# Two ways to the expert activations: half of the tokens by gathered rows, half by dense plain products, and the up product in a stage of its own

## The chip, the cores and the metric

One core of a Trainium2 chip runs the whole program. The metric is the device time of one execution in microseconds, the median of three runs. Four engines compute (PE is TensorE, DVE is VectorE, ACT is ScalarE, POOL is GpSimd), SP is the queue that issues DMA transfers, and each engine executes its own instructions in order and waits on semaphores.

## The reference

The reference is three layers on x [256 tokens, 1024]: a first block (attention, then an expert layer), and two mixers with windowed attention. Only the expert layer is touched. For one token with normalised row h it computes, for each of 8 heads:

```
q      = h @ w_query                          # 2 halves of 128 per head
sc     = q . sub_keys                         # 128 scores per half
top 16 of each half -> 256 pair sums -> top 16 of them: (expert, score)
gates  = softmax(best 16 scores)
act    = gelu(h . expert_down[expert])        # rows of 1024
out   += sum gates * act * expert_up[expert]
```

There are 16384 experts (128 x 128), and 8 x 16 = 128 chosen ones ("slots") for each token. expert_down and expert_up are 64 MB each in fp32.

## The kernel before, in words

It never gathers. It treats the experts as 128 chunks of 128 rows. For every chunk and all 256 tokens it computes the dense activations gelu(down_chunk . h), multiplies them by a table of gates that is zero where a token did not choose the expert, and adds weights x up_chunk into four PSUM banks. The transposed normalised rows are `whole` (fp32, [128, 8, 256]) and `hT` (the same split in a high and a low fp32r part). `plain` products are fp32 matmuls; `three_passes` (L228) replaces one fp32 product by three fp32r ones of high and low parts.

The expert layer runs in three parts, each a block with a barrier between.

`route_phase` (L1379): 16 steps, one for each head half. PE makes the queries (three passes over 8 k-blocks, L1468) and the scores (L1480); ACT and POOL split the query weights; DVE takes the top 16 of each half straight from PSUM (`top16`, L1521), both token halves (t = 0 and 1) in one step. After the steps DVE takes the top 16 of the pair sums for each head (L1542), finds the two digits of each chosen expert by comparing with 16 candidates (L1560 to L1578) and normalises the gates. Under this PE runs `EARLY` = 24 dense chunks in plain fp32 (class `Ahead`, L1278: 8 matmuls with 256 columns for a chunk).

`spread_phase` (L1599): the slots are transposed, and for 32 groups of 8 tokens DVE builds two one-hot matrices of [128 slots, 8, 128] (L1661, L1664), PE multiplies them token by token (L1706) and thereby scatters the gates into [128, 128] tables, ACT copies them out, and DVE merges them with the chunks whose activations exist. PE runs 14 more plain chunks in between.

`experts_phase` (L1733): the up products of all 128 chunks (`add`, L1777: 12 matmuls with 512 columns: two token halves, two halves of D, three passes). For the first 38 chunks the activations exist. For the other 90 (`both`, L1793) PE also makes the down product in three passes, 24 matmuls with 256 columns, whose operands ACT and DVE split; ACT applies gelu and DVE multiplies by the gates. Every chunk also needs ACT and DVE to split 1024 columns of the up rows (L1813, L1843).

All loads go out of SP's queue in program order: a down chunk as two halves of 256 KB into two buffers, an up chunk in the same way. POOL issues no DMA.

After it the two mixers run as they are; they are not touched.

## Time and profile before

| | |
|---|---|
| median of 3 runs | 1572.26 us (1571.95 to 1572.6) |
| profiled execution | span 1569.9 us; its whole time is not shown, so the 2.4 us between span and median are taken as what lies around it |
| PE busy | 1531.3 us, 98% of the span |
| DVE busy | 1013.8 us, 65% |
| ACT busy | 699.4 us, 45% |
| POOL busy | 42.0 us, 3% |
| DMA | 239.30 MB, mean 152 GB/s |
| granted PE clock | 1.00 in nearly all of the span (mean 0.999) |

A busy PE is one with a matmul in flight, not one at its peak. Shares are over the whole span; the stages of the expert layer are told apart by time below.

### The profile page before, as it was taken

The numbers are of one execution on the slowest core, as the hardware profiler recorded it, in microseconds if no ns is written. First come the engines' busy times: TensorE is split into PE (matmuls) and PEld (weight loads), VectorE is DVE, ScalarE is ACT, GpSimd is POOL, SyncE is SP. The second block draws the span as 40 slices with busy tenths as digits, with TensorE's granted clock in tenths as the row PEclk, the third lists the DMA queues.
The fourth block names the chain that finished last, engine by engine and source line by source line (L and its number), as shares of the span: only waits on it lengthen the run. The fifth ranks groups of instructions, "written<-read, shape, count | busy, mean of one in ns | idle before, by whom it ended". The sixth has DMA issues, their size and how long they took to land. (4 is left out here: it accounts for less than half of the span.)

```text
span 1569.9 us, 29197 instructions
## 1 busy us (share of the span) xinstructions
PE 1531.3 (98%) x9047; PEld 1338.6 (85%) x9047; DVE 1013.8 (65%) x2452; ACT 699.4 (45%) x1484; POOL 42.0 (3%) x42
## 2 busy tenths in 40 slices
PE   7998999999999999999999999999999999999998
PEld 4665798889878899999999999979999999759994
DVE  4666589989867666666666666665555555247762
ACT  2443241223344444444444444446666666326651
POOL 0000260000000000000000000000000000000000
PEclk9999999999999999999999999999999999999999
DMA  7420244422265555555555555557544444317630
GB/s 290 157 105 1 65 145 146 150 86 68 82 205 189 187 187 187 187 187 187 187 187 187 187 187 187 187 174 229 175 149 148 148 147 148 94 33 231 168 106 28
DMA packets 163511, 239.30 MB, mean 152 GB/s; under 512 B 41712, under 2 KB 91376, under 8 KB 161904
## 3 DMA queue, kind: packets, MB, share of 16 engines
q1 hardware_dynamic: 163440, 238.42, 46.8%
q8 instruction: 37, 0.61, 0.2%
q14 instruction: 34, 0.28, 0.1%
HBM read 237.09 MB, written 1.29 MB: 152 GB/s over the span
## 5 line engine op out<-in xcount | busy, mean ns | idle before, releaser
L232 PE MATMUL projection<-hT_high,down_low 128*128 128x256 f32 x720 | 203.8, 283 | 0.0
L231 PE MATMUL projection<-hT_low,down_high 128*128 128x256 f32 x720 | 203.7, 283 | 0.0
L230 PE MATMUL projection<-hT_high,down_high 128*128 128x256 f32 x720 | 203.3, 282 | 0.0
L230 PE MATMUL experts_acc<-experts_uh,experts_wh 128*128 128x512 f32 x512 | 200.6, 392 | 2.5 <-DVE experts_ul L1843 2.5
L231 PE MATMUL experts_acc<-experts_ul,experts_wh 128*128 128x512 f32 x512 | 200.3, 391 | 0.0
L232 PE MATMUL experts_acc<-experts_uh,experts_wl 128*128 128x512 f32 x512 | 199.2, 389 | 0.0
L1813 ACT ACTIVATE experts_uh<-whole 128x512 fp32r<-128x512 f32 x256 | 146.9, 624 | 58.5 <-PE experts_acc L232 52.4
L1843 DVE TENSOR_TENSOR experts_ul<-whole,experts_uh 128x512 fp32r<-128x512 f32 x256 | 164.7, 684 | 2.5 <-ACT experts_uh L1813 2.5
L1849 DVE TENSOR_TENSOR experts_full<-experts_full,spread 128x256 f32<-128x256 f32 x90 | 38.3, 426 | 168.5 <-ACT experts_full L1365 168.5
L230 PEld LDWEIGHTS projection<-hT_high,down_high 128*128 128x128 f32 x720 | 137.9, 191 | 3.5
L231 PEld LDWEIGHTS projection<-hT_low,down_high 128*128 128x128 f32 x720 | 137.9, 191 | 3.5
L232 PEld LDWEIGHTS projection<-hT_high,down_low 128*128 128x128 f32 x720 | 137.9, 191 | 0.0
L1300 PE MATMUL plain_u<-whole,down_raw 128*128 128x256 f32 x608 | 136.6, 379 | 0.4 <-PEq L1385 0.4
L1341 ACT ACTIVATE down_high<-down_raw 128x512 fp32r<-128x512 f32 x180 | 112.6, 633 | 46.9 <-DMA down_raw<-in_downT 46.3
L1365 ACT ACTIVATE experts_full<-projection 128x256 f32<-128x256 f32 x90 | 34.5, 384 | 219.9 <-PE projection L232 219.9
L230 PE MATMUL mix_a_pj<-mix_a_wh,hT_high 128*128 128x384 f32 x368 | 129.1, 351 | 0.0
L1300 PEld LDWEIGHTS plain_u<-whole,down_raw 128*128 128x128 f32 x608 | 113.1, 190 | 14.7 <-issue 0.7
L232 PE MATMUL mix_a_pj<-mix_a_wh,hT_low 128*128 128x384 f32 x368 | 123.5, 336 | 0.0
L231 PE MATMUL mix_a_pj<-mix_a_wl,hT_high 128*128 128x384 f32 x368 | 123.5, 335 | 0.0
L1348 DVE TENSOR_TENSOR down_low<-down_raw,down_high 128x512 fp32r<-128x512 f32 x180 | 115.8, 684 | 2.8 <-ACT down_high L1341 2.8
L230 PEld LDWEIGHTS experts_acc<-experts_uh,experts_wh 128*128 128x128 f32 x512 | 96.5, 188 | 21.0 <-DVE experts_ul L1843 1.9
L232 PEld LDWEIGHTS experts_acc<-experts_uh,experts_wl 128*128 128x128 f32 x512 | 96.2, 188 | 20.7
(392 smaller groups left out, 2982.2 us busy)
## 6 DMA issues: line engine op xcount, KB each, us to landing
down_raw<-in_downT SPq DMA_DIRECT2D x256, 256.0 KB, 3.5
whole<-in_up SPq DMA_DIRECT2D x256, 256.0 KB, 2.8
mix_raw<-in_wa SPq DMA_DIRECT2D x46, 768.0 KB, 6.1
block_w_raw<-in_w SPq DMA_DIRECT2D x16, 768.0 KB, 6.2
mix_raw<-in_wb SPq DMA_DIRECT2D x16, 768.0 KB, 6.6
route_raw<-in_route SPq DMA_DIRECT2D x16, 576.0 KB, 3.8
wo<-in_wo SPq DMA_DIRECT2D x4, 1024.0 KB, 8.3
mix_a_w_gate<-in_wa SPq DMA_DIRECT2D x8, 512.0 KB, 7.9
```

Of the source, the lines that this page charges most:

```text
L230: pe.matmul(out, lhs[0], rhs[0], start=start, stop=False, skip_group_check=True)
L231: pe.matmul(out, lhs[0], rhs[1], start=False, stop=False, skip_group_check=True)
L232: return pe.matmul(out, lhs[1], rhs[0], start=False, stop=stop, skip_group_check=True)
L1300: mm = pe.matmul(self.u[b][:, 0:SEQ], self.raw[b][:, k, :], self.h[:, k, :], start=k == 0, stop=k == KD - 1, skip_group_check=True)
L1341: act.activation(self.high[b][:, self.half(h)], self.raw[b][:, self.half(h)], ACT.Copy).then_inc(self.highs, 1)
L1348: eng.tensor_tensor(self.low[b][:, k], self.raw[b][:, k], self.high[b][:, k].bitcast(F32), ALU.subtract).then_inc(self.lows, 1)
L1365: act.activation(into, self.u[b][:, 0:SEQ], ACT.Gelu).then_inc(self.done, 1)
L1813: act.activation(uh[b][:, w], raw_u[b][:, w], ACT.Copy).then_inc(u_high, 1)
L1843: dve.tensor_tensor(ul[b][:, w], raw_u[b][:, w], uh[b][:, w].bitcast(F32), ALU.subtract).then_inc(u_low, 1)
L1849: dve.tensor_tensor(full[:], full[:], spread[:, n - READY, :], ALU.mult)
```

## The change

Tokens 0 to 127 (t = 0) no longer use dense down products. DVE finishes their selection first, computes expert numbers, and POOL gathers, for each of the 128 slots, one row of `peer_down` for each token ([128 tokens, 1024], 512 KB) by an indirect DMA into a ring of 10 buffers that lie in the not yet used half of the table. DVE multiplies each with the token's normalised row and sums (`dots`). The 128 dots are placed between the pieces of DVE's other work.

Tokens 128 to 255 (t = 1) get all 128 chunks in plain fp32 with 128 columns, into PSUM banks that hold four chunks, so that one gelu covers 512 columns. Chunks come as one load of 512 KB into a ring of 6. 48 of them stand before the transposes, 2 after each of the 16 groups of t = 1, 40 after, and 8 among the 16 groups of t = 0. The gates of t = 0 are multiplied by their activations before they are spread, so its groups need no merge.

Route, spread and selection become one block; scores are saved by ACT to SBUF. The up products are a stage of their own with 128 equal chunks, loads of 512 KB into a ring of 4, and splits of 1024 columns in one instruction.

The diff, cut to what the steps below speak of (`halves`, `pairs` and `indices` do for one token half what the loops at L1536 to L1578 did for both, in the same instructions):

```diff
-EARLY = 24
-LATE = 14
-BEFORE_GATE = 16
-LEAD = 8
 FINE = 8
-READY = EARLY + LATE
-REST = 1
+RING = 6
+FIRST_FREE = 4
+UP_RING = 4
+GATHERS = 10
+BEFORE = 48
+BESIDE = 32
+TAIL = 8
+WAITING = BESIDE // 4
+DOTS_FIRST, DOTS_HALVES, DOTS_PAIRS, DOTS_INDEX, DOTS_TURN, DOTS_GROUP = 6, 2, 3, 4, 2, 2
...
+        "down_rows": a["peer_down"][0],
         "up": a["peer_up"][0].reshape(NKEYS, NKEYS, D),
...
+    def load(self, sp, n):
+
+        b = self.buffer(n)
+        sp.dma_start(self.raw[b][:, 0:KD, :], self.down[n]).then_inc(self.landed[b], 16)
...
+    def half(self, pe, n, h):
+
+        b, g, i = self.buffer(n), n // 4, n % 4
+        if h == 0:
+            pe.wait_ge(self.landed[b], (n // RING + 1) * 16)
+            if i == 0:
+                wait(pe, self.taken, g - 1)
+        for k in range(KD // 2 * h, KD // 2 * (h + 1)):
+            mm = pe.matmul(self.u[g % 2][:, i * P:(i + 1) * P], self.raw[b][:, k, :], self.h[:, k, P:SEQ], start=k == 0,
+                           stop=k == KD - 1, skip_group_check=True)
+        if h == 1:
+            mm.then_inc(self.projected, 1)
...
+    gathered = [sparse[:, b * D:(b + 1) * D] for b in range(GATHERS)]
+    after_ring = sparse[:, GATHERS * D:]
+    w_high, w_low = [[nc.alloc_sbuf_tensor_at(f"select_{n}{b}", [P, KD, P], F32R, offset=table_at + 4 * D * (GATHERS + 2 * i + b))
+                      for b in range(2)] for i, n in enumerate(("w_high", "w_low"))]
...
+            for n in range(RING - FIRST_FREE):
+                chunks.load(sp, n)
+            for hp in range(NW, HP):
+                sp.wait_ge(s_ready, hp - NW + 1)
+                sp.dma_start(raw[hp % NW][:], weights[hp]).then_inc(landed_q[hp % NW], 16)
+            for n in range(RING - FIRST_FREE, NKEYS):
+                if n < RING:
+                    sp.wait_ge(s_ready, HP - NW + chunks.buffer(n) + 1)
+                else:
+                    sp.wait_ge(chunks.projected, n - RING + 1)
+                chunks.load(sp, n)
+            for n in range(UP_RING):
+                sp.wait_ge(chunks.projected, NKEYS - RING + n + 1)
+                sp.dma_start(raw[n][:, 0:KD, :].rearrange("p k c -> p (k c)"), d["up"][n]).then_inc(up_in[n], 16)
...
+            for s in range(SLOTS):
+                if s % PART == 0:
+                    pool.wait_ge(chosen, s // PART + 1)
+                wait(pool, dotted, s - GATHERS + 1)
+                pool.indirect_dma_start(gathered[s % GATHERS], None, d["down_rows"],
+                                        bass.IndirectOffsetOnAxis(ap=expert[:, s:s + 1], axis=0)).then_inc(gather_in[s % GATHERS], 16)
...
+            def spread(t, g):
+                m = t * GROUPS + g
+                pe.wait_ge(a_one_ready, m + 1)
+                pe.wait_ge(a_two_ready, m + 1)
+                wait(pe, g_kept, m - 1)
+                wait(pe, merged, min(m - 1, GROUPS))
+                for q in range(Q):
+                    mm = pe.matmul(gp[m % 2][:, q, :], a_two[m % 2][:, q, :], a_one[m % 2][:, q, :], start=True, stop=True)
+                mm.then_inc(g_ready, 1)
+            for hp in range(HP):
+                queries(hp)
+                if hp > 0:
+                    scores_of(hp - 1)
+            scores_of(HP - 1)
+            for n in range(BEFORE):
+                chunks.project(pe, n)
+            for t in (1, 0):
+                for n, src in enumerate((index[1], coarse, fine)):
+                    mm = columns(t, n, src, (1, 2, 3)[n])
+                if t == 1:
+                    mm = columns(1, 3, gate, 4)
+                mm.then_inc(cols_turned, 1)
+            for g in range(GROUPS):
+                spread(0, g)
+                for n in range(BESIDE // GROUPS):
+                    chunks.project(pe, BEFORE + g * (BESIDE // GROUPS) + n)
+            for n in range(BEFORE + BESIDE, NKEYS - TAIL):
+                chunks.project(pe, n)
+            columns(0, 3, gate, 5).then_inc(cols_turned, 1)
+            for g in range(GROUPS):
+                spread(1, g)
+                if g % 2 == 1:
+                    chunks.project(pe, NKEYS - TAIL + g // 2)
 
...
+            def save(hp):
+                act.wait_ge(s_ready, hp + 1)
+                act.activation(saved[:, hp, :], sp_[hp % 2][:, 0:SEQ], ACT.Copy).then_inc(s_saved, 1)
...
+            save(HP - 1)
+            for g in range(BEFORE // 4):
...
+            late = BEFORE // 4
+            for g in range(GROUPS):
+                t = slice(g * Q, (g + 1) * Q)
+                act.wait_ge(g_ready, g + 1)
+                act.activation(table[:, 1, BEFORE:, t], gp[g % 2].rearrange("p q i -> p i q")[:, BEFORE:], ACT.Copy).then_inc(g_kept, 1)
+                if (g + 1) * (BESIDE // GROUPS) // 4 > g * (BESIDE // GROUPS) // 4:
+                    chunks.gelu(act, late, late_gelu[late - BEFORE // 4])
+                    late += 1
+            for g in range(late, (NKEYS - TAIL) // 4):
+                n = g - BEFORE // 4
+                wait(act, freed, n - WAITING + 1)
+                chunks.gelu(act, g, late_gelu[n % WAITING])
+            act.wait_ge(dots_done, 1)
+            act.activation(act_u[:], u[:], ACT.Gelu).then_inc(u_ready, 1)
+            for g in range(GROUPS):
+                m = GROUPS + g
+                act.wait_ge(g_ready, m + 1)
+                act.activation(table[:, 0, :, g * Q:(g + 1) * Q], gp[m % 2].rearrange("p q i -> p i q"), ACT.Copy).then_inc(g_kept, 1)
+                if g % 8 == 7:
+                    chunks.gelu(act, (NKEYS - TAIL) // 4 + g // 8, tail_gelu[g // 8])
...
+            def dots(lo, hi):
+
+                for s in range(lo, hi):
+                    b = s % GATHERS
+                    dve.wait_ge(gather_in[b], s // GATHERS * 16 + 16)
+                    dve.tensor_tensor_reduce(gathered[b], gathered[b], h_row[:], 1.0, 0.0, ALU.mult, ALU.add, u[:, s:s + 1]).then_inc(dotted, 1)
...
+            def onehots(t, g):
+                m = (1 - t) * GROUPS + g
+                wait(dve, g_ready, m - 1)
+                dve.tensor_tensor(a_one[b].rearrange("p q (h l) -> p q h l", l=FINE),
+                                  coarse_of[n % 2][:, q].unsqueeze(3).broadcast_to([P, Q, COARSE, FINE]),
+                                  fine_of[n % 2][:, q].unsqueeze(2).broadcast_to([P, Q, COARSE, FINE]), ALU.mult).then_inc(a_one_ready, 1)
+                dve.tensor_tensor(a_two[b], sbt["iota"][:].unsqueeze(1).broadcast_to([P, Q, P]),
+                                  slotT[:, t, 0, g * Q:g * Q + Q].unsqueeze(2).broadcast_to([P, Q, P]),
+                                  ALU.is_equal).then_inc(a_two_ready, 1)
+                if g % BATCH < 3 and n + 1 < BATCHES:
+                    digit(t, n + 1, g % BATCH)
...
+            def merge(g):
+                t = slice(g * Q, (g + 1) * Q)
+                dve.wait_ge(g_kept, g + 1)
+                dve.tensor_tensor(table[:, 1, 0:BEFORE, t], table[:, 1, 0:BEFORE, t], gp[g % 2].rearrange("p q i -> p i q")[:, 0:BEFORE],
+                                  ALU.mult).then_inc(merged, 1)
+
+            def join(g, other):
+
+                rows = dense[:, g * 512:(g + 1) * 512]
+                dve.wait_ge(g_kept, GROUPS)
+                dve.wait_ge(chunks.taken, g + 1)
+                dve.tensor_tensor(rows, rows, other, ALU.mult).then_inc(freed, 1)
...
+            for h in range(0, HEADS_P, 2):
+                halves(0, h)
+                halves(0, h + 1)
+                pairs(0, h)
+                if h % 4 == 2:
+                    indices(0, h // 4)
+                    choose(h // 4)
+            dve.wait_ge(gain_in, 16)
+            dve.scalar_tensor_tensor(h_row[:], x[:, 0, :], sbt["root"][:, 0:1], gain_row, ALU.mult, ALU.mult)
+            dve.drain()
+            at = DOTS_FIRST
+            dots(0, at)
+            for h in range(0, HEADS_P, 2):
+                for i in range(2):
+                    halves(1, h + i)
+                    dots(at, at + DOTS_HALVES)
+                    at += DOTS_HALVES
+                pairs(1, h)
+                dots(at, at + DOTS_PAIRS)
+                at += DOTS_PAIRS
+                if h % 4 == 2:
+                    indices(1, h // 4)
+                    dots(at, at + DOTS_INDEX)
+                    at += DOTS_INDEX
             for t in range(NT):
...
+            dots(at, at + DOTS_TURN)
+            at += DOTS_TURN
+            dve.wait_ge(cols_turned, 2)
...
+                    onehots(1, g)
-                        join(n)
+                dots(at, at + DOTS_GROUP)
+                at += DOTS_GROUP
+            first, last = BEFORE // 4, (NKEYS - TAIL) // 4
+            beside = (BEFORE + BESIDE) // 4
+            for g in range(first, beside):
+                join(g, late_gelu[g - first])
+            left = SLOTS - at
+            for n, g in enumerate(range(beside, last)):
+                dots(at + left * n // (last - beside), at + left * (n + 1) // (last - beside))
+                join(g, late_gelu[(g - first) % WAITING])
+            dve.drain().then_inc(dots_done, 1)
+            for part in range(2):
+                digit(0, 0, part)
+            dve.wait_ge(u_ready, 1)
+            dve.tensor_tensor(gate[:, 0, :], gate[:, 0, :], act_u[:], ALU.mult).then_inc(cols_ready, 1)
+            dve.wait_ge(cols_turned, 3)
+            dve.tensor_copy(slotT[:, 0, 3], slots[:, 0, 3])
+            digit(0, 0, 2)
             for g in range(GROUPS):
-                wait(act, joined, n - 1)
...
         def sem(n):
             return c.enter_context(nc.semaphore(f"experts_{n}"))
-        uh, ul = [[sb(f"{n}{b}", [P, D], F32R) for b in range(2)] for n in ("uh", "ul")]
-        wh, wl = [[sb(f"{n}{b}", [P, SEQ], F32R) for b in range(2)] for n in ("wh", "wl")]
+        uh, ul = [[v[:].rearrange("p k t -> p (k t)")[:, b * D:(b + 1) * D] for b in range(2)] for v in hT]
+        raw_u = [v[:, 0:KD, :].rearrange("p k c -> p (k c)") for v in raw]
...
+            def load(n, b):
+                sp.wait_ge(u_low, n - (UP_RING - 1))
+                sp.dma_start(raw_u[b], up[n]).then_inc(up_in[b], 16)
...
                 pe.wait_ge(wgt_ready, n + 1)
+                pe.wait_ge(u_low, n + 1)
-                    pe.wait_ge(u_low, n * 2 + (h + 1))
...
-                for h, w in enumerate(halves):
-                    act.wait_ge(up_in[b][h], (n - b) * 8 + 16)
-                    act.activation(uh[b][:, w], raw_u[b][:, w], ACT.Copy).then_inc(u_high, 1)
+                act.wait_ge(up_in[b], (n - b) * (16 // UP_RING) + 16)
+                act.activation(uh[b % 2], raw_u[b], ACT.Copy).then_inc(u_high, 1)
...
                 wait(dve, added, n - 1)
-                dve.tensor_copy(wh[b][:], src)
+                dve.tensor_copy(wh[b % 2][:], table[:, :, n, :])
-                dve.tensor_tensor(wl[b][:], src, wh[b][:].bitcast(F32), ALU.subtract).then_inc(wgt_ready, 1)
-                for h, w in enumerate(halves):
-                    dve.wait_ge(u_high, n * 2 + (h + 1))
-                    dve.tensor_tensor(ul[b][:, w], raw_u[b][:, w], uh[b][:, w].bitcast(F32), ALU.subtract).then_inc(u_low, 1)
```

## Rows read from the trace of the kernel before

**Rows 1.** The page: its first line, and transfers of down rows.
```profile
span 1569.9 us, 29197 instructions
...
down_raw<-in_downT SPq DMA_DIRECT2D x256, 256.0 KB, 3.5
```

**Rows 2.** Windows (from:to, length, busy us, PE clock, DMA share, GB/s) of the expert stages.
```profile
187.00:235.00 48.00, 47.77 (x399) 47.52 (x399) 39.60 (x230) 21.33 (x41) 34.17 (x28) 1.00 0.47 151
...
235.00:317.00 82.00, 82.00 (x381) 72.20 (x380) 75.19 (x199) 15.93 (x30) 0.00 (x0) 1.00 0.45 148
...
325.00:424.00 99.00, 98.86 (x697) 93.41 (x696) 95.29 (x126) 30.96 (x88) 0.00 (x0) 1.00 0.19 61
...
440.00:530.00 90.00, 90.00 (x399) 74.51 (x397) 64.78 (x135) 39.57 (x70) 0.00 (x0) 1.00 0.57 194
...
535.00:1034.00 499.00, 499.00 (x3207) 455.79 (x3206) 315.10 (x621) 236.82 (x443) 0.00 (x0) 1.00 0.56 184
```

**Rows 3.** PE's timeline (start us, length us, count) at the expert layer's joints.
```profile
340.99 1.95 PE L1706 MATMUL spread_g<-spread_a 128*128 128x128 f32 x16
...
424.09 2.02 PE L1706 MATMUL spread_g<-spread_a 128*128 128x128 f32 x16 [0.23 <-issue]
...
429.28 0.47 PE L230 MATMUL experts_acc<-experts_uh,experts_wh 128*128 128x512 f32 x1 [0.63 <-DVE experts_ul L1843]
...
1040.97 2.39 PE L238 MATMUL projection<-ident 128*128 128x128 f32 x20
```

**Rows 4.** DVE's timeline in the selection.
```profile
190.78 0.50 DVE L1526 MAX8 route_topv<-route_sp 128x8 f32<-128x128 f32 x2 [0.72 <-PE route_sp L1480]
...
234.03 0.50 DVE L1526 MAX8 route_topv<-route_sp 128x8 f32<-128x128 f32 x2 [0.41 <-PE route_sp L1480]
...
240.51 0.75 DVE L1545 TENSOR_TENSOR route_cand<-route_topv 128x256 f32<-128x256 f32 x2
...
245.70 0.76 DVE L1545 TENSOR_TENSOR route_cand<-route_topv 128x256 f32<-128x256 f32 x2
...
283.71 2.29 DVE L1568 TENSOR_TENSOR route_match<-route_partf,iota 128x2048 f32<-128x2048 f32 x1
...
290.81 2.29 DVE L1568 TENSOR_TENSOR route_match<-route_partf,iota 128x2048 f32<-128x2048 f32 x1
...
312.84 0.29 DVE L1580 TENSOR_SCALAR route_eighth<-route_index 128x256 f32<-128x256 f32 x1
```

**Rows 5.** DVE's timeline: a multiply and sum over 1024 columns, and one-hots.
```profile
4.96 1.23 DVE L1259 CUSTOM_DVE_ANT_0 open_sq<-x 128x1024 f32<-128x1024 f32 x1 [4.96 <-DMA x<-in_x]
...
6.11 0.08 DVE L1259 DVE_READ_ACCUMULATOR2_ANT open_ssum<- 128x1 f32 x1
...
341.02 1.21 DVE L1661 TENSOR_TENSOR spread_a<-spread_coarse_of,spread_fine_of 128x1024 f32<-128x1024 f32 x1
...
342.16 1.22 DVE L1664 TENSOR_TENSOR spread_a<-iota,spread_i 128x1024 f32<-128x1024 f32 x1
```

**Rows 6.** DVE and ACT timelines in the up products.
```profile
455.93 1.16 ACT L1813 ACTIVATE experts_uh<-whole 128x512 fp32r<-128x512 f32 x2 [1.65 <-PE experts_acc L232]
...
455.97 0.29 DVE L1838 CAST experts_wh<-early 128x256 fp32r x1 [0.72 <-PE experts_acc L232]
...
456.68 1.29 DVE L1843 TENSOR_TENSOR experts_ul<-whole,experts_uh 128x512 fp32r<-128x512 f32 x2
...
458.69 0.29 DVE L1838 CAST experts_wh<-early 128x256 fp32r x1 [0.73 <-PE experts_acc L232]
```

**Rows 7.** Windows where DMA is busiest.
```profile
8.00:24.00 16.00, 14.54 (x59) 9.56 (x58) 10.46 (x41) 4.43 (x12) 0.99 (x2) 1.00 1.02 409
...
1045.00:1050.00 5.00, 4.37 (x40) 4.18 (x39) 3.41 (x14) 1.78 (x2) 0.00 (x0) 1.00 1.00 342
```

**Rows 8.** Windows with an idle PE.
```profile
0.00:20.00 20.00, 11.53 (x49) 8.23 (x50) 12.38 (x47) 6.04 (x12) 2.18 (x8) 1.00 0.93 337
...
1415.00:1420.00 5.00, 2.79 (x12) 2.77 (x12) 4.32 (x11) 0.93 (x1) 0.00 (x0) 0.73 0.97 244
```

More of the change, by code:

```diff
@@ L1504, in one @@
+            for hp in range(HP):
+                if 2 <= hp + 1 < HP:
+                    weight_high(hp + 1)
                 act.wait_ge(q_ready, hp + 1)
                 wait(act, s_ready, hp - 1)
-                steps_in = ahead.u[b] if isinstance(hp, int) and hp < 2 else qp[b % 2]
-                act.activation(qh[b % 2][:], steps_in[:, 0:SEQ], ACT.Copy).then_inc(q_kept, 1)
-            second_row_high(act, hT, whole, row_high)
-            steps(act, one)
-            def early_chunk(n, b):
-                ahead.gelu(act, n, b, early[:, n, :])
@@ L1988, in build @@
[L1988 to L1995 removed]
+                table_at = -(-nc.sbuf_base // 32) * 32
```

594 lines of the change are left out of this document (202 added, 392 removed).

## The prediction

> **What bounds the kernel now.** First the page: a span of 1569.9 us [rows 1]. Then the windows by stage, the timelines of PE and DVE at the joints, and the windows with the busiest DMA. PE is busy all the time: 47.77 of 48 us in the routing steps, 82.00 of 82 beside the selection, 98.86 of 99 in the spread, all of 440 to 530 (up products alone) and all of 535 to 1034 (down and up products together) [rows 2]. In the spread DVE is nearly as full, 95.29 of 99. DMA runs at 61 to 198 GB/s. So the expert layer is bound by PE, from 187 us to its last up product at 1040.97 [rows 3], and later stages are untouched. I carry the sum as the shift of that end, and the median of 1572.26 as the profiled time (span plus 2.4 us).
>
> **Up products as a stage of their own.** The windows give 399/12 = 33.25 chunks in 90 us, 2.71 us each [rows 2]; DVE's conversions of the weights come 2.72 us apart (455.97, 458.69) [rows 6]. 128 x 2.72 = 348.2 us. The old fused loop cost 499/(3207/36) = 5.60 us a chunk. Merging the half splits into whole ones is priced at zero: ACT's pair ends at 457.09, DVE's whole split (1.15 to 1.3 us) then ends at 458.3 to 458.4, and PE starts its next chunk near 458.6. The cover is 0.2 us; a lateness of d costs d/2 for each chunk, so 0.2 us would be 13 us. I take none.
>
> **Routing steps.** Unchanged on PE, one in (234.03-190.78)/13 = 3.33 us [rows 4]. ACT's saving of scores (0.4 us) comes before the next weight split, and POOL is busy 34.17 of 48 us [rows 2], so there is slack: zero, at most 0.8 us a step if it had none (13 us).
>
> **DVE from 187 to the first dot.** One half with both tokens, or two halves with one, is (240.51-234.03-0.34)/2 = 3.07 us (the 0.34 is a conversion between them); the pairs of one head with both tokens, or two heads with one, 5.19 us; the comparisons take 7.10 us for 128 slots and one digit, so 64 slots and two digits 7.3 with more fixed cost, plus small ones: 8.5 [rows 4]. For t = 0: the eighth score is saved at about 211.5 (190.78 + 6 x 3.33 + 0.8), then 3.1 + 5.2 + 8.5 + 0.6 gives the first 64 expert numbers at 229; four heads more (4 x 3.07 of halves, 2 x 5.19 of pairs, 9.1 of digits and numbers) end at 261. POOL's gathers stand behind its weight splits, so they begin near 231.5. The row of h takes 1.3. A dot is the multiply and sum over 1024 columns: the accumulator is read 1.15 us after the start and takes 0.08 [rows 5]; 1.22 us. Six dots: 269.5.
>
> **To the transposes.** t = 1 takes 8 x 3.07 + 4 x 5.19 + 2 x 8.5 = 62.4 us, with 2 x 8 + 3 x 4 + 4 x 2 = 36 dots of 43.9: 375.8. Small instructions like those from 312.84 on [rows 4] 3.4, two dots 2.4, copies and digits about 3.4: first one-hots at 385. PE meanwhile needs 48 chunks. A chunk is 16 instructions of 128x128, as a spread group is: 1.95 us with its own tail [rows 3], and half of the 256-column rate (82/381 x 16/2 = 1.72) from below [rows 2]; 1.79. 48 x 1.79 = 86, so PE, free at 235, is done by 321 if loads keep up, and idles; this cover makes DVE the bound of this stretch.
>
> **Groups of t = 1.** For each, one-hots 2 x 1.14 (341.02 to 342.16) [rows 5], digits 0.3, a merge of 384 columns about 0.5 (estimated from 1.14 us for 1024), two dots 2.44. 16 of them with two dots more: 91 us. PE has 3 x 1.79 = 5.4 of the 5.6 us, plus 3 us at half clock after its idling. 385 + 91 + 3 = 479.
>
> **The remaining 50 dots.** DVE has 50 x 1.22 + 20 joins x 0.6 = 73 us, PE 40 x 1.79 = 72. But now transfers decide. A gather and a chunk are 0.524 MB each. With 10 gathers and 6 chunks ahead, 40 gathers must still land, and if the engines serve both queues alike, 40 chunks land with them: 80 x 0.524 = 42 MB. The opening shows 409 GB/s sustained over 16 us at a full share [rows 7]: 102 us. In the groups 4 x 0.524 MB in 5.6 us is 374 GB/s, just under it; before that 92 blocks in 150 us are 321. So the last dot is at 581, not 552.
>
> **Groups of t = 0.** Gelu, the multiply, transpose, copy, digit and first one-hots: 5 us. PE then has 24 x 1.79 = 43 and DVE 42; PE starts at half clock: +3. From the last spread group's end to the first up product lay 429.28-426.11 = 3.2 us [rows 3], and a last join adds 0.5. In all 54.5 us, so the first up product is at 635.5 instead of 429.28, and the last ends at 635.5 + 348.2 = 983.7 instead of 1041: a gain of 57 us. **1515 us.**
>
> The unknown with no row is the POOL gather. Its issue costs at least nothing visible (10 in flight hide it) and the nearest row is a whole transfer of 256 KB on SP's queue, 3.5 us to landing [rows 1]. Up to 102/40 = 2.5 us for each it is hidden. I take it as hidden: it is an issue, not a landing, and queued ones overlap.
>
> **Rivals.**
>
> DVE-bound (15%): gathers get the larger part of DMA, the chunks catch up beside the groups of t = 0. The last dot is at 552: 1486 us. For it: PE asks for only 0.524/1.79 = 293 GB/s. Against: 40 gathers in 73 us leave only 120 of 409 GB/s to the chunks, and the joins wait for chunk 119.
>
> Slower DMA (17%): 342 GB/s is what the start of the first mixer shows at a full share [rows 7]. Then a group of t = 1 takes 6.13 us (+8) and the 80 blocks 123 us (+21): 1544 us. For it: rows scattered over 64 MB. Against: that window moves shorter rows, the opening's are 4 to 6 KB like the gathered ones. The Trainium skill ("DMA: Bandwidth & Descriptors", Where 436 GB/s comes from) puts what HBM gives one core at about 358 GB/s, by which the 80 blocks would take 117 us and the time be about 1533; the 409 GB/s of the opening speak against that ceiling for a core that streams alone.
>
> Half clock (6%): PE waits for loads in each chunk. The granted clock fell to 0.73 on average in a window with PE busy 2.79 of 5 us [rows 8]. A chunk at half clock is 3.58 us: 48 of them end at 407 (+24) and the 36 before the last dots take 129 + 6 us (+33): 1572, no change. Against: in the opening PE was busy 11.53 of 20 us at a clock of 1.00 [rows 8], and the waits here are 0.6 to 0.8 us each. The Trainium skill ("TensorE: Matmul & The Clock Gate", HAM oscillation — how this bites in real kernels) tells of just this loop, a short burst of matmuls and a wait for the next transfer, falling back to half clock in each round; the opening's window says that pauses of this kind need not.
>
> Slow gathers (16%), the one on the other side: POOL needs 3.5 us to issue one, alone or because DVE, always busy, holds it up. 128 x 3.5 = 448 from 231.5, last dot near 683, +102: 1617 us. It decides from (581+57-231.5-3)/128 = 3.15 us on. For it: nothing in the trace shows POOL's transfers, and all 128 go through it one by one. Against: DVE's load here is two-operand arithmetic, during which nothing else has been seen to stop. The Trainium skill ("SBUF — State Buffer", Who interferes with whom) lists copies, casts and tensor_scalar as the instructions that lock out POOL's descriptor writing and counts tensor_tensor as harmless for it; no run here shows either.
>
> **Numbers.** Forecast 46%, own range 1498 to 1532. The range of 8 in 10 takes in the DVE-bound case, slow DMA with up to 13 us for the uncovered splits, and stops at the half-clock case: 1480 to 1574. Two tenths of a per cent (3 us) is about what a measurement of this kernel tells from no change. Faster 0.80 (forecast, DVE-bound, slow DMA, and a tail of the others), same 0.03, slower 0.17.
>
> **What would show it.** DVE's first one-hot of t = 1 near 385 and last dot near 581; PE idle before the transposes; DMA near 400 GB/s between 479 and 581 and DVE's dots waiting for gathers there; up chunks 2.72 us apart with DVE's splits ending before PE asks; granted clock at 1.00 but for the two restarts; POOL's gathers issued well under 2.5 us apart when buffers are free. Wrong would be: gathers evenly spaced at over 3 us with free buffers, up chunks over 2.8 us apart, or a clock at half through the chunks.

## The result: faster by 1.7%, less than half of the forecast gain

| | before | after |
|---|---|---|
| median | 1572.11 us (1571.35 to 1572.6) | 1545.76 us (1543.71 to 1547.66) |
| ratio | | 0.9833, 95% interval 0.9819 to 0.9847 |
| profiled execution, span | 1569.9 us | 1544.3 us |

The gain is 26 us; the forecast was 57 (1515 us). The time lies inside the stated range and on the side forecast, but next to the figure of the rival "slower DMA", so each step has to be looked at. The page after, its first line, the busy totals, the gathers and the dots (count | busy us, mean ns | idle before):

```profile
span 1544.3 us, 24562 instructions
...
PE 1405.4 (91%) x8327; PEld 1203.9 (78%) x8327; DVE 1038.5 (67%) x2332; ACT 557.5 (36%) x1049; POOL 212.1 (14%) x170
...
L1417 POOL DMA_INDIRECT table<-in_down_rows,select_expert x128 | 168.9, 1320 | 174.8 <-DVE select_u L1604 143.9
L1604 DVE CUSTOM_DVE_ANT_0 table<-table,h_row 128x1024 f32<-128x1024 f32 x128 | 152.5, 1223 | 44.3 <-DMA table<-in_down_rows,select_expert 42.0
```

PE is no longer the engine that is always busy: it has 1405 of 1544 us, where it had 1531 of 1570. The gathers cost POOL 1.32 us each, and 143.9 of the 174.8 us that POOL idles before them are waits for a dot to free a buffer: the POOL queue has room. The windows (length, busy us of PE, PEld, DVE, ACT, POOL, PE clock, DMA share, GB/s), which answer to [rows 2]:

```profile
235.00:330.00 95.00, 80.43 (x649) 76.34 (x649) 87.47 (x275) 7.64 (x12) 37.50 (x32) 0.96 0.99 382
330.00:388.00 58.00, 17.09 (x130) 15.05 (x128) 54.29 (x163) 2.89 (x4) 26.86 (x22) 0.68 0.77 289
388.00:485.00 97.00, 90.88 (x795) 90.91 (x796) 94.17 (x137) 17.31 (x25) 58.99 (x36) 0.95 0.94 355
485.00:500.00 15.00, 14.18 (x125) 13.80 (x124) 15.00 (x27) 1.19 (x2) 9.94 (x6) 1.00 1.03 409
500.00:595.00 95.00, 63.00 (x493) 57.10 (x492) 52.79 (x86) 4.78 (x8) 35.63 (x35) 0.94 1.00 398
595.00:650.00 55.00, 46.94 (x386) 46.03 (x387) 46.48 (x52) 18.03 (x20) 0.00 (x0) 0.89 0.18 58
660.00:1000.00 340.00, 340.00 (x1458) 269.65 (x1457) 235.65 (x365) 128.51 (x122) 0.00 (x0) 1.00 0.60 187
```

Read from the top, the bound moves from stage to stage. DVE's selection sets 235 to 388: it is busy 87.47 of 95 us and then 54.29 of 58. Up to 330 DMA is full too (share 0.99), and from 290 on PE waits 0.5 us for most chunks: its last of the 48 ends at 346, where the forecast had 321. From there to 384 PE idles, and from 330 to 388 DMA has a share of only 0.77. DVE still sets the groups, 94.17 of 97. From 485 on DMA is full and sets the pace: PE has 63 of 95 us, DVE 53. Then comes the tail (the groups of t = 0), and from 660 PE alone. PE's timeline at the joints between the stages, to be read beside [rows 3]:

```profile
383.78 0.48 PE L1451 MATMUL select_slots<-ident,select_columns_of 128*128 128x128 f32 x1 [37.74 <-DVEq L1677]
...
597.40 0.48 PE L1451 MATMUL select_slots<-ident,select_gate 128*128 128x128 f32 x1 [19.22 <-DVE select_gate L1720]
...
652.31 0.77 PE L235 MATMUL experts_acc<-hT_high,experts_wh 128*128 128x512 f32 x1 [1.53 <-DVE hT_low L1819]
...
657.99 0.40 PE L236 MATMUL experts_acc<-hT_low,experts_wh 128*128 128x512 f32 x1
...
1013.74 2.39 PE L243 MATMUL experts_idle<-ident 128*128 128x128 f32 x20
```

The last up product ends at 1013.74 instead of 1040.97 [rows 3]: 27.2 us, and what follows it is unchanged within 2 us. So the whole question is why this point is 30 us later than the 983.7 forecast. DVE's timeline, the first one-hots of tokens 128 to 255 and dots near the end:

```profile
391.61 1.23 DVE L1625 TENSOR_TENSOR select_a_one<-select_coarse_of,select_fine_of 128x1024 f32<-128x1024 f32 x1
...
577.66 1.23 DVE L1604 CUSTOM_DVE_ANT_0 table<-table,h_row 128x1024 f32<-128x1024 f32 x1 [1.33 <-DMA table<-in_down_rows,select_expert]
...
580.22 1.23 DVE L1604 CUSTOM_DVE_ANT_0 table<-table,h_row 128x1024 f32<-128x1024 f32 x1 [1.32 <-DMA table<-in_down_rows,select_expert]
...
594.14 1.23 DVE L1604 CUSTOM_DVE_ANT_0 table<-table,h_row 128x1024 f32<-128x1024 f32 x1
```

Each dot waits for its gather, and they come 2.56 us apart: two transfers of 0.524 MB at 409 GB/s, one gather and one chunk. From the groups' end to the last dot's end DMA moved this much (the windows as above):

```profile
482.20:581.00 98.80, 79.98 (x641) 73.70 (x639) 61.28 (x103) 6.57 (x11) 47.39 (x42) 1.00 1.03 409
581.00:595.40 14.40, 0.00 (x0) 0.00 (x0) 9.71 (x18) 0.00 (x0) 0.00 (x0) 0.57 0.81 323
```

That is 98.8 us x 409 and 14.4 us x 323 GB/s, 45 MB or 86 transfers, where the forecast had 80. Then the up stage: DVE's conversion of the weights, once a chunk, where [rows 6] had 2.72 us:

```profile
674.87 0.29 DVE L1815 CAST experts_wh<-table 128x256 fp32r x1 [0.59 <-PE experts_acc L237]
...
677.67 0.29 DVE L1815 CAST experts_wh<-table 128x256 fp32r x1 [0.51 <-PE experts_acc L237]
...
680.49 0.29 DVE L1815 CAST experts_wh<-table 128x256 fp32r x1 [0.60 <-PE experts_acc L237]
```

It is 2.80 us now, with PE busy 340 of 340 us. This time from chunk to chunk is called the period below. DVE waits for PE, not the other way: each of the 12 matmuls of a chunk starts 0.2333 us after the one before instead of 0.2267.

The steps of the forecast beside the trace, in us:

| step | forecast | measured | adds |
|---|---|---|---|
| first one-hots of t = 1 | 385 | 391.6 | 6.6 |
| from there to the last group's dots (482.2) | 94 | 90.6 | -3.4 |
| from there to the last dot's end (595.4) | 102 | 113.2 | 11.2 |
| tail to the first up product (652.31) | 54.5 | 56.9 | 2.4 |
| up stage | 348.2 | 361.4 | 13.2 |
| sum | | | 30.0 |

### The profile page after: what moved, and what is told of

It reads as the page before. It is cut to its first block and busy times, and to the rows that moved or that the text cites. A ratio compares the mean times of both kernels' runs of the same rounds, so it can differ in the third digit from the quotient of the medians.

```text
span 1544.3 us, 24562 instructions
## 1 busy us (share of the span) xinstructions
PE 1405.4 (91%) x8327; PEld 1203.9 (78%) x8327; DVE 1038.5 (67%) x2332; ACT 557.5 (36%) x1049; POOL 212.1 (14%) x170
## 5 line engine op out<-in xcount | busy, mean ns | idle before, releaser
L1310 PE MATMUL plain_u<-whole,ring 128*128 128x128 f32 x2048 | 250.7, 280 | 32.1 <-DMA ring<-in_downT 26.3
L1310 PEld LDWEIGHTS plain_u<-whole,ring 128*128 128x128 f32 x2048 | 238.0, 194 | 42.8 <-DMA ring<-in_downT 36.1
L1803 ACT ACTIVATE hT_high<-ring 128x1024 fp32r<-128x1024 f32 x128 | 135.7, 1061 | 224.9 <-PE experts_acc L237 223.8
L235 PE MATMUL experts_acc<-hT_high,experts_wh 128*128 128x512 f32 x512 | 204.3, 399 | 1.5 <-DVE hT_low L1819 1.5
L237 PE MATMUL experts_acc<-hT_high,experts_wl 128*128 128x512 f32 x512 | 203.4, 397 | 0.0
L236 PE MATMUL experts_acc<-hT_low,experts_wh 128*128 128x512 f32 x512 | 203.3, 397 | 0.0
L1417 POOL DMA_INDIRECT table<-in_down_rows,select_expert x128 | 168.9, 1320 | 174.8 <-DVE select_u L1604 143.9
L1604 DVE CUSTOM_DVE_ANT_0 table<-table,h_row 128x1024 f32<-128x1024 f32 x128 | 152.5, 1223 | 44.3 <-DMA table<-in_down_rows,select_expert 42.0
L1819 DVE TENSOR_TENSOR hT_low<-ring,hT_high 128x1024 fp32r<-128x1024 f32 x128 | 156.8, 1225 | 27.4 <-ACT hT_high L1803 27.4
L236 PEld LDWEIGHTS experts_acc<-hT_low,experts_wh 128*128 128x128 f32 x512 | 97.0, 189 | 17.8
L1460 PE MATMUL select_four<-select_a_one,select_a_two 128*128 128x128 f32 x512 | 66.2, 287 | 10.5 <-DVE select_a_two L1628 10.3
```

What stands on the lines that cost most here:

```text
L235: pe.matmul(out, lhs[0], rhs[0], start=start, stop=False, skip_group_check=True)
L236: pe.matmul(out, lhs[0], rhs[1], start=False, stop=False, skip_group_check=True)
L237: return pe.matmul(out, lhs[1], rhs[0], start=False, stop=stop, skip_group_check=True)
L1310: mm = pe.matmul(self.u[g % 2][:, i * P:(i + 1) * P], self.raw[b][:, k, :], self.h[:, k, P:SEQ], start=k == 0, stop=k == KD - 1, skip_grou ...
L1417: pool.indirect_dma_start(gathered[s % GATHERS], None, d["down_rows"], bass.IndirectOffsetOnAxis(ap=expert[:, s:s + 1], axis=0)).then_inc( ...
L1460: mm = pe.matmul(gp[m % 2][:, q, :], a_two[m % 2][:, q, :], a_one[m % 2][:, q, :], start=True, stop=True)
```

## The experiments

Three questions: what slows the up products, what sets the last dots, and what PE's half clock costs. "After" is the changed kernel; ratios are to the kernel before, with 95% intervals. From e5 on most runs stand on a base, named in their expectations. e9, e11, e12 and e13 were executed twice each, the others four or five times. Code is cut to the lines that matter, and periods and times of dots are those of the profiled execution. Among four runs with 48 chunks ahead and no other change that touches the dots (after, e1, e2, e16) the last dot starts between 592.9 and 595.4, which is the spread to keep in mind.

**e1, weights moved (and only they).**
```
+        sb("align", [P, 24])                      # 96 bytes ahead of wh, wl
         wh, wl = [[sb(f"{n}{b}", [P, NT, P], F32R) ...
```


> The up stage ran 2.80 us a chunk (matmul starts 0.2333 us apart) where the fused kernel had 2.72 (0.2267), with PE never idle. In the changed kernel the split gate weights wh and wl start 32 bytes past a multiple of 128 bytes in each partition (address 213664); in the kernel before they start on a multiple of 128 (223872). This run puts 96 bytes ahead of them and changes nothing else. Theory (address of the stationary operand): starts 0.2267 apart, 2.72 us a chunk, 128 x 0.08 = 10 us less, about 1536. Rival (whole-width splits on ScalarE and VectorE, or operands in hT, or the loop of four): still 0.2333 and 2.80, time within 1 us of 1545.8.


1546.0 us, 0.9818 (0.9805 to 0.9832); period 2.80. The alignment of the weights taken by itself is not it.

**e2, half splits again.**
```
+                for h in range(2):
+                    act.activation(uh[b % 2][:, w], raw_u[b][:, w], ACT.Copy).then_inc(u_high, 1)
```


> Each up chunk is split in two halves of 512 again, with PE waiting for each half, as before the change; operands stay where they are. Rival (the whole-width splits beside the matmuls slow them): 0.2267 us between matmuls, 2.72 a chunk, about 1536. Theory (operand address): still 0.2333 and 2.80, the time within 2 us of 1545.8; the only gain is that the first chunk starts some 1 us earlier.


1541.6 us, 0.9791 (0.9777 to 0.9805); period 2.80. The whole-width splits don't slow the matmuls. The 4 us are more than the 2 expected: the first up product is at 650.4 instead of 652.3, and 8 instead of 13 of them start at half clock.

**e3, 56 chunks ahead.** `BEFORE = 56` instead of 48.


> 56 chunks instead of 48 are projected ahead of the transposes, in the 38 us in which PE was idle and DMA at 0.77 of its time (289 GB/s). Theory (from 388 us on the last dot is set by bytes over the shared DMA): 8 chunk loads of 0.524 MB leave the stretch behind the transposes, 4.2 MB at 400 GB/s = 10.5 us, so the last dot comes near 584 instead of 594, time about 1536. Rival (dots are paced by VectorE or by their own queue): last dot within 2 us of 594, time 1545. Second rival (the 8 loads slow the gathers of the selection, so the one-hots start later): first one-hot of tokens 128 to 255 after 394 instead of 391.6, and the gain is under 5 us.


1534.3 us, 0.9751 (0.9737 to 0.9764); last dot at 582.1. The theory holds that bytes set the last dot: it comes 12.0 us earlier for 10.5 expected, and the median is 11.4 lower.

**e4, fillers.**
```
+            for s in range(SLOTS - 7, SLOTS + 1):
+                pe.wait_ge(dotted, s)
+                keep_clock(pe, slots[:, 1, 0, :], sbt["ident"][:], 16)
             columns(0, 3, gate, 5).then_inc(cols_turned, 1)
...
+            keep_clock(pe, slots[:, 1, 0, :], sbt["ident"][:], 16)
```


> Filler matmuls keep TensorE busy where it sat idle around the t = 0 groups: 16 after each of the last 8 dots, 16 after the last dense chunk, 20 instead of 3 at the start of the up stage. Granted clock was 0.50 from 581 to about 606 and from 651 to 657.6. Theory: the clock stays at 1.00, the first 13 up matmuls take 0.233 instead of 0.427 us apart (2.5 us) and the first spreads 3.7 instead of 6.3 us, 3 to 5 us in all, about 1542. Rival (those stretches are paced by VectorE, fillers too few or only in the way): within 1 us of 1545.8.


1557.8 us, 0.9909 (0.9894 to 0.9924): slower by 12 us. PE's timeline of this run:

```profile
578.25 30.48 PE L243 MATMUL select_slots<-ident 128*128 128x128 f32 x256 [3.10 <-DVE select_u L1608]
608.57 0.27 PE L1451 MATMUL select_slots<-ident,select_gate 128*128 128x128 f32 x1
```

128 fillers are 256 records and 30.48 us: one is 0.24 us, where I had reckoned with half of it. The last dot was done at 592.7 and the transpose came at 608.57, 14 us later than it would follow a dot in the changed kernel. No up product started at half clock; the price was the fillers' own.

**e5 to e8, on a base with e3's 56 chunks and e2's half splits.** e5 widens the routing root tile by 120 bytes so that ring, table and weights move to multiples of 128 bytes; e6 allocates two PSUM banks ahead of the accumulators; e7 gives the high halves buffers of their own and also moves the weights 96 bytes on; e8 has 4 fillers a dot, 7 and 9 at the joint. The base by itself was not run; its 1530 us are a sum.
```
-  sb("root", [P, NT], c=c0)            +  sb("root", [P, 32], c=c0)                       # e5
+  idle, _ = [... psum_tensor(f"experts_idle{b}", [P, 512], F32) ... for b in range(2)]   # e6, ahead of acc
+  sb("align", [P, 24])      ahead of wh, wl, and                                          # e7
+  uh = [sb(f"uh{b}", [P, D], F32R)[:] for b in range(2)]                                  # e7
```


> Base of this and the next three: 56 chunks ahead of the transposes and half splits together (about 1530: 1534.3 and 1541.6 alone, gains of 11.4 and 4.1 taken as adding). Here the routing root tile is widened so that the ring (raw up rows, written by DMA, read by ScalarE and VectorE), the table and the split weights start on multiples of 128 bytes; they started 32 past one. Theory A (misaligned accesses beside the matmuls slow the moving reads): matmul starts 0.2267 apart, 1520. Rivals (PSUM banks, place of the operands, the program's loop): 0.2333, 1530.


1527.3 us, 0.9717 (0.9701 to 0.9733); period 2.788.


> Base (56 ahead, half splits) with the accumulators in PSUM banks 2 to 5, as in the kernel before, instead of 0 to 3. Theory B (the bank that is written sets the pace): 0.2267 apart, 1520. Rivals: 0.2333, 1530.


1530.8 us, 0.9739 (0.9723 to 0.9755); period 2.80. Not the banks.


> Base (56 ahead, half splits) with the high halves of the up rows in buffers of their own at addresses 217856 and 221952, where the kernel before had them near, instead of hT at 25728; the low halves stay in hT at 33920. Theory C (the place of the moving operand): the passes that read the high half start the next matmul 0.2267 later, those that read the low half 0.2333, 12 x 128 x 2/3 x 0.0067 = 7 us less, 1523. Rivals: 0.2333 throughout, 1530.


1531.7 us, 0.9742 (0.9726 to 0.9758); period 2.80. Moving the high halves alone brings nothing.


> Base (56 ahead, half splits) with fewer fillers than in the run that became slower: there one filler took 0.24 us of TensorE, not 0.12, and 128 of them after the dots delayed the last transpose by 14 us. Now 4 after each of the last 8 dots (0.95 of 2.56 us), 7 after the last dense chunk (1.65 us of 1.75 idle), 9 at the start of the up stage (2.1 us). Theory (half clock at the first spreads and first up matmuls costs 2 to 5 us): clock 1.00 from the first spread on, 1526 to 1528, and less spread between executions. Rival: 1530, as the base.


1532.3 us, 0.9749 (0.9733 to 0.9765): nothing gained. PE had idled 17.43 us before the first filler, the clock was already down, and the 32 fillers, 0.32 us each, ran until 586.5, past the last dot's end at 584.9.

e5 gave two things. The period fell by 0.012 us, and DMA, with both queues streaming, rose. POOL's window 500 to 545 in e6 and then in e5:

```profile
500.00:545.00 45.00, 24.44 (x23) 1.00 1.03 409
```
```profile
500.00:545.00 45.00, 22.85 (x22) 1.00 1.03 419
```

In this window the runs whose ring and gather buffers start 32 bytes past a multiple of 128 give 409 or 410 GB/s (after, e1 to e4, e6 to e8, e16), those on multiples of 128 (e5, e9, e11, e12, e14, e15, e17, e18) 419.

**e9 to e12.** e9, e11 and e12 stand on e5; e10 is the kernel before.
```
+  sb("align", [P, 96])       # e9: 384 bytes ahead of wh, wl
+  sb("align", [P, 8])        # e10: 32 bytes ahead of wh, wl, in the kernel before
+  raw_u = [spare[:]... for b in (0, 1, 0, 1)]   and loads of 512 columns     # e11
+  uh, ul in ring buffers 4 and 5, h_row and one new buffer                    # e12
```


> Base of e9, e11 and e12: 56 chunks ahead, half splits, ring and table aligned (1527.3, up period 2.788 us). Here the split weights move 384 bytes on, so that weights and up rows have the same address modulo 1024, as in the kernel before. Theory D (relation of the two addresses): period 2.72, about 1518. Rivals: 2.788, 1527.


1518.5 us, 0.9657 (0.9629 to 0.9685); period 2.72. DVE's timeline of e9, and then of e5, which differs from it by the 384 bytes alone:

```profile
806.32 0.29 DVE L1818 CAST experts_wh<-table 128x256 fp32r x1 [0.72 <-PE experts_acc L237]
...
809.04 0.29 DVE L1818 CAST experts_wh<-table 128x256 fp32r x1 [0.72 <-PE experts_acc L237]
...
811.76 0.29 DVE L1818 CAST experts_wh<-table 128x256 fp32r x1 [0.72 <-PE experts_acc L237]
```
```profile
804.07 0.30 DVE L1817 CAST experts_wh<-table 128x256 fp32r x1 [0.80 <-PE experts_acc L237]
...
806.86 0.29 DVE L1817 CAST experts_wh<-table 128x256 fp32r x1 [0.79 <-PE experts_acc L237]
...
809.64 0.29 DVE L1817 CAST experts_wh<-table 128x256 fp32r x1 [0.79 <-PE experts_acc L237]
```

> The kernel before with its split weights wh and wl put 32 bytes further, so that they start 32 past a multiple of 128 as in the changed kernel. Theory A (alignment of the stationary operand): the up products start 0.2333 us apart, 12 x 128 x 0.0067 = 10 us more, 1582. Rivals: 0.2267, 1572.


1577.7 us, 1.0034 (1.0018 to 1.0050): 5.6 us of the 10 expected. PE's timeline of it, in the stretch of up products alone:

```profile
479.98 0.40 PE L232 MATMUL experts_acc<-experts_uh,experts_wl 128*128 128x512 f32 x1
480.21 0.40 PE L230 MATMUL experts_acc<-experts_uh,experts_wh 128*128 128x512 f32 x1
480.44 0.40 PE L231 MATMUL experts_acc<-experts_ul,experts_wh 128*128 128x512 f32 x1
480.68 0.40 PE L232 MATMUL experts_acc<-experts_uh,experts_wl 128*128 128x512 f32 x1
```

0.70 us for three: the slow pace, put into the kernel before by 32 bytes. Between down products it costs less (from 564 us on a pair of chunks takes 11.31 us instead of 11.24), hence 38 x 0.08 + 90 x 0.035 = 6.2 us.

> The raw up rows go back to whole, two buffers, in loads of 256 KB a half, as in the kernel before; the first load then waits for the end of the selection, some 3 us. Theory E (ring writes or 512 KB loads beside the matmuls): period 2.72, 1527 + 3 - 9 = 1521. Rivals: 2.788, 1530.


1532.8 us, 0.9748 (0.9717 to 0.9780); period 2.788. Neither the ring nor the size of the loads.


> All split up rows leave hT: the high halves lie in the two ring buffers that the up stage does not use, the low halves in h_row and a buffer at 217856, everything on multiples of 128 bytes. Theory C (the place of the moving rows, all of them): period 2.72, about 1518. Rivals: 2.788, 1527.


1520.4 us, 0.9669 (0.9641 to 0.9698); period 2.72. This looks like a hit for "place of the rows", but the new places (69376, 73984, 209664, 217856) have 256 as the remainder of a division by 512, as the weights at 213760 have. So it is a second case of e9's relation, with other addresses, and e5 (rows 128, weights 256) and e11 are the two without it. In the kernel before rows and weights both have 128.

**e13, half of each chunk load.** From the seventh chunk on the kernel leaves out the second half of each load, so its activations are not those of the reference.
```
+        k = KD if n < RING else KD // 2
+        sp.dma_start(self.raw[b][:, 0:k, :], self.down[n][:, 0:k, :])...
```


> The changed kernel, but from the seventh chunk on only half of each down chunk is loaded (the other half keeps what the buffer held; this part of the computation is changed): 122 x 0.262 MB = 32 MB less, 80 us of DMA at 400 GB/s. Theory (dots after 500 us wait for bytes that they share with the chunk loads): dots come 1.9 us apart or less instead of 2.56, the last one 25 to 40 us earlier, about 1512 (1505 to 1520), and then TensorE's chunks or VectorE set it. Rival (the gathers' own queue or the waits around the ring of ten): still 2.56 apart, 1545.


1521.7 us, 0.9679 (0.9659 to 0.9698), just outside the 1505 to 1520 expected; last dot at 569.7, 24 us earlier. DVE's timeline:

```profile
518.94 1.23 DVE L1605 CUSTOM_DVE_ANT_0 table<-table,h_row 128x1024 f32<-128x1024 f32 x1 [0.74 <-DMA table<-in_down_rows,select_expert]
...
520.89 1.23 DVE L1605 CUSTOM_DVE_ANT_0 table<-table,h_row 128x1024 f32<-128x1024 f32 x1 [0.71 <-DMA table<-in_down_rows,select_expert]
...
522.86 1.23 DVE L1605 CUSTOM_DVE_ANT_0 table<-table,h_row 128x1024 f32<-128x1024 f32 x1 [0.73 <-DMA table<-in_down_rows,select_expert]
```

1.96 us apart instead of 2.56: with fewer bytes and as many transfers the dots come faster, so in the changed kernel bytes set them. The 1.96 is 0.524 + 0.262 MB at 402 GB/s (the window 500 to 560), but bytes are not the only bound left. POOL's timeline in e13, and then in the changed kernel:

```profile
519.31 1.67 POOL L1418 DMA_INDIRECT table<-in_down_rows,select_expert  x1 [0.30 <-issue]
521.29 1.64 POOL L1418 DMA_INDIRECT table<-in_down_rows,select_expert  x1 [0.30 <-issue]
```
```profile
471.47 1.68 POOL L1417 DMA_INDIRECT table<-in_down_rows,select_expert  x1 [1.07 <-DVE select_u L1604]
473.46 1.97 POOL L1417 DMA_INDIRECT table<-in_down_rows,select_expert  x1 [0.30 <-issue]
...
517.79 0.94 POOL L1417 DMA_INDIRECT table<-in_down_rows,select_expert  x1 [1.62 <-DVE select_u L1604]
520.35 0.94 POOL L1417 DMA_INDIRECT table<-in_down_rows,select_expert  x1 [1.62 <-DVE select_u L1604]
```

In e13 POOL issues one gather straight after another, one in 1.96 us, with its buffer free for some 9 us: POOL's own pace has become a bound beside DMA's. In the changed kernel, from 515 on, it mostly waits for a dot to free one. The issue itself takes 0.94 us while DVE idles (517.79, 520.35) and mostly 1.68 or 1.97 while DVE runs dots or one-hots (471.47, 473.46). So e13 shows that bytes set the 2.56, not how the two queues would share DMA if their transfers differ.

**e14, e15, e16.** e14: `BEFORE = 64`, `GATHERS = 9`, scratch moved, on e9. e15: `TAIL = 0`, and
```
+            sp.wait_ge(dotted, SLOTS - 4)        # ahead of the first up loads
```
e16: `sb("align", [P, 120])` ahead of wh, wl in the changed kernel.


> On e9 (1518.5): 64 chunks ahead of the transposes instead of 56, with a gather ring of 9 instead of 10 to make room for routing scratch. TensorE idles some 20 us there in the run with 56 and DMA is at 0.91. If bytes set the last dot, up to 0.09 x 58 us = 5 us of DMA time is filled: last dot near 579 instead of 583, about 1514. Rival (loads and gathers already fill DMA when TensorE has work, or nine buffers slow the gathers): 1518 to 1520.


1511.4 us, 0.9618 (0.9602 to 0.9634). Last dot at 573.8, where e9 has it at 580.7: 7 us for the 5 expected. PE's windows of e3 and of e14 (PE busy, clock, DMA share, GB/s), for the same stretch:

```profile
330.00:388.00 58.00, 28.36 (x214) 0.80 0.88 343
```
```profile
330.00:388.00 58.00, 46.91 (x374) 0.98 1.02 416
```

48, 56 and 64 chunks ahead: 289, 343, 416 GB/s here, and last dots at 594.1, 582.1, 573.8 (the last with the aligned ring).


> On e9 (1518.5): no dense chunks behind the last dots. All 128 are projected before the t = 0 groups, in the 29 us that TensorE idled; the first up loads wait until 124 dots are done. Two more chunk loads stand before the last dot (+2.6 us); the tail loses VectorE's wait of 4.4 us for the last GELU and becomes VectorE's alone, 2.3 to 2.7 us a group against 2.68. Net -3, about 1515. Rival (the up loads, no longer early, delay the up stage, or half clock makes the spreads of 3.2 us the bound): 1519 to 1525.


1516.4 us, 0.9643 (0.9627 to 0.9660), 2 of 3 us. The tail is DVE's alone: PE now has a short wait before each spread, where it had two spreads and a chunk back to back:

```profile
625.74 2.02 PE L1461 MATMUL select_four<-select_a_one,select_a_two 128*128 128x128 f32 x16 [0.24 <-issue]
628.01 2.02 PE L1461 MATMUL select_four<-select_a_one,select_a_two 128*128 128x128 f32 x16 [0.25 <-issue]
```

> The changed kernel with nothing but 480 bytes ahead of the split weights, so that they start at 214144, equal to the up rows' 25728 and 33920 modulo 512 (both 128); ring and table stay 32 bytes off. Theory D: period 2.72 us a chunk, 1545.8 - 10 = 1536. Rival (ring and table count as well): 2.79 to 2.80, 1545.


1540.1 us, 0.9802 (0.9779 to 0.9825); period 2.769. Between the two: with ring and table 32 bytes off, equal remainders give 4 of the 10 us of the stage; e9, with ring and table aligned as well, has all of them.

**e17, e18: the parts together.**


> e9 with both: 64 chunks ahead and no dense chunks in the tail. The last dot came at 573.8 us with 64 ahead; two more chunk loads before it add 2.5 us, so 576.3; the tail to the up stage was 50.2 us (583.5 to 633.7) instead of 53.7 (574.9 to 628.6). Sum 576.3 + 1.2 + 50.2 = 627.7 for the up stage's start instead of 628.6: 1510.5, within 1 us of 1511.4 (the gains don't add). Rival (they add, -7.1 - 2.1 against 1518.5): 1509.


1510.0 us, 0.9608 (0.9595 to 0.9621): the two overlap, as summed.


> e14 (64 ahead, tail as it was) with three dots a group instead of two beside the 16 groups. VectorE was busy 95.7 of 97 us there, so a group takes 1.15 us more (5.8 to 6.9) and the groups end 18 us later; but gathers and chunk loads then fill DMA (3 + 2 transfers of 0.524 MB in 6.9 us), and the last dot is set by bytes: at most 6 us earlier, 1506 to 1511. Rival (TensorE's 24 chunks behind the groups, at 2.5 us beside the gathers, become the last to end, or DMA has less to do while groups are slower): 1511 to 1518.


1508.4 us, 0.9593 (0.9580 to 0.9606), last dot at 569.5. This is the fastest version, 37 us under the changed kernel. Its window of the groups:

```profile
388.00:485.00 97.00, 80.54 (x680) 78.47 (x681) 96.43 (x138) 13.82 (x22) 61.44 (x42) 0.97 0.96 366
```

## Why the prediction was right in parts and wrong in others

**Right in mechanism: the last dots.** The forecast had DMA deciding after the groups, both queues served alike, 2.5 us for each pair. Measured were 2.56 us, and e13 showed that it is bytes. The DVE-bound rival fell (its last dot was 552). The half-clock rival fell too: from 500 to 560 PE worked 2.05 us on a chunk and waited 0.51 for the next load, and the granted clock stayed at 1.00.

"Slow gathers" fell as well: with buffers free and DVE idle POOL issued a gather in 0.94 us, not 3.5, and never in more than 1.99. But one reason given against it does not hold. The forecast said that beside DVE's two-operand arithmetic nothing had been seen to stop. The Trainium skill ("SBUF — State Buffer", Who interferes with whom) names copies, casts and tensor_scalar as what locks POOL out, and the dots and one-hots are none of these. The trace agrees only in part: no gather stopped for long, but beside dots and one-hots most took 1.68 to 1.99 us. In the groups, DVE busy 94 of 97 us, 36 of them took 1.65 us on average. It cost nothing here, since POOL waited for buffers. It would count as soon as bytes allow a gather in less than 2 us, as in e13.

**Wrong in size: the last dot, 14 us late (6.6 - 3.4 + 11.2).** The failed step is "the remaining 50 dots". It took "10 gathers and 6 chunks ahead" as given at the groups' end, hence 80 transfers or 42 MB. By the windows above DMA moved 45 MB, 86 transfers, before the last dot: at 409 GB/s 8 us more. The other 3 us are the last four dots, which DVE still had to do when the bytes were in. The buffers were not all full because the groups moved 355 GB/s and not the 374 of the forecast; over 97 us this is 3.5 of the 6 missing transfers; where the others come from is not shown. "To the transposes" was 6.6 us short as well (391.6 for 385); how much of this reached the last dot was not isolated.

Beside this the forecast overlooked a gain. It had PE idling after its 48 chunks and called this cover for DVE's bound. It was not free: all rows have to come through DMA before the last dot, so what is not moved at 350 us is moved at 590. From 330 to 388 DMA stood at 289 GB/s, since PE asked for nothing; by the shares that is (0.99 - 0.77) x 58 = 13 us of DMA. e3 and e14 show it: 8 chunks moved there brought the last dot forward by 12 us with nothing else changed, 16 by 20 us (e14's base also has the 419 GB/s of the aligned ring, and e14 one gather buffer fewer). This was in the forecast's own sum and is not what made it wrong.

**Wrong: the up stage, 13 us, in two terms.** First, "128 x 2.72": the step took a period that belongs to where the tensors lie. 1523 matmuls at 0.2333 instead of 0.2267 us are 10.1 us. e9 and e12 give 2.72 back, e5 and e11 don't, e10 puts part of the loss into the kernel before. The matmuls are the same in all of them. I had looked for the risk in the uncovered splits (0.2 us a chunk); e2 shows that it was not there. Second, the first 13 up products ran at a granted clock of 0.50, 0.43 us apart instead of 0.23, after PE's waits of 1.75 and 1.53 us at the joint: 2.7 us. The forecast had restarts at half clock at two places, not at this one. This second term is partly chance: e3, e13 and e16 have the same two waits in their profiles, and there the first up products start 0.23 us apart.

The Trainium skill ("SBUF — State Buffer", Who interferes with whom) gives TensorE two independent read ports, one for the moving operand and one for the weight load. Read by this alone, the relation of their addresses should not matter. The measurement decides: with the rows' remainder equal to the weights' 2.72 us a chunk, with 128 bytes between them 2.788, PE never idle in either.

**Right: the tail** (56.9 for 54.5; the terms given for it add up to 54.7) **and the groups** (90.6 for 94). **A wrong rival with the right figure:** the "slower DMA" case forecast 1544 us, but its mechanism, 342 GB/s because of scattered rows, is refuted: 409 and even 419 GB/s were sustained with both queues streaming. That its figure was met is luck. The ceiling of about 358 GB/s for one core, which the forecast quoted from the Trainium skill ("DMA: Bandwidth & Descriptors", Where 436 GB/s comes from), did not bind this core, which streams alone.

**What stays open.** Which modulus counts in the addresses (256 or 512 would both fit; 128 is excluded, since e5 has all on multiples of 128), by what mechanism, why ring and table 32 bytes off take part of the gain away (e16), and why e7, in which the high halves had the weights' remainder and the low halves not, with the ring 32 bytes off, gained nothing at all. What decides at the joint whether the clock falls is open too; the waits alone don't. That fillers placed exactly there would bring back the 2.7 us was not isolated; e4 and e8 changed other places with it.

## What to carry to other kernels

When a stage is going to be bound by bytes, sum all bytes from the first moment at which they could be moved to the moment at which the last is needed: an earlier stretch where DMA idles "under cover" of another engine is paid for at the end. And don't take every buffer as full when the stage begins: 6 missing transfers were 8 us here. When a period is carried over from one kernel to another, it is carried with the placement of its operands: 32 to 128 bytes of shift between weights and moving rows made 3% of a stage in which TensorE never waited. A filler has a price too, and one that must wait for an event is worth less than none when it runs past it.

## What the runs showed of the hardware that was not expected

- TensorE, 128x512 fp32r passes at full clock (2.4 GHz): starts 0.2267 us apart with weights and rows at equal remainders modulo 512 and everything on multiples of 128 (before, e9, e12); about 0.2323 (2.788/12) when the remainders differ by 128 (e5, e11); 0.2333 with the weights 32 bytes past a multiple of 128, be the buffers of raw rows and gates aligned (e10) or not (after), and also with the weights aligned, a remainder different by 128 and ring and table 32 bytes off (e1). At a granted clock of 0.50 (1.2 GHz) the same passes started 0.427 apart, which is 512 columns at 1.2 GHz with nothing over.
- One core's DMA with two queues streaming 4 KB rows: 409 or 410 GB/s into buffers 32 bytes past a multiple of 128, 419 into aligned ones.
- An indirect gather of 128 rows of 4 KB takes POOL 0.94 us to issue while DVE idles and mostly 1.68 to 1.99 beside dots and one-hots, 1.32 on average. It does not slow the dots beside it (1.223 us, as in [rows 5]).
- Two queues, SP's and POOL's, with transfers of the same size share DMA in equal parts while both have work: from 515 to 565 a dot and a chunk both come every 2.56 us. How they share when the sizes differ is not shown, since in e13 POOL's own pace was a bound too.
